# Attention A of a two-block transformer kernel: scores with the keys on partitions, plain fp32 values on column halves, values in portions of two key tiles

## What is computed

```python
qa = axial_rope(rms_norm(qa.reshape(b, s, A_HEADS, HEAD_DIM), q_norm_a), ...)
ka = axial_rope(rms_norm(ka.reshape(b, s, A_KV_HEADS, HEAD_DIM), k_norm_a), ...)
def block(qi):
    sc = jnp.einsum('bqkgd,bskd->bkgqs', qi, k).astype(jnp.float32) * scale
    p = jax.nn.softmax(sc, axis=-1).astype(v.dtype)
    return jnp.einsum('bkgqs,bskd->bqkgd', p, v)
oa = dense_gqa_attention(...) * jax.nn.silu(ga)
```

## Time and profile before

| | us |
|---|---|
| median of the runs | 2344.59 |
| the profiled execution | 2350.09 |
| its span, first to last instruction | 2348.8 |
| attention A, from its first matmul to the first of `pe_b_proj` | 190.0 |
| `pe_b_proj`, to the first matmul of attention B | 32.4 |

### The profile page before, as it was taken

How to read it: one execution, slowest core, us unless ns; L and a number is a source line. 1 busy time by engine, 2 the same in 40 slices (tenths; PEclk the granted TensorE clock), 3 DMA queues, 4 the chain that set the end, 5 groups by cost and what they waited for, 6 DMA issues and landing times.

```text
span 2348.8 us, 31548 instructions
## 1 busy us (share of the span) xinstructions
PE 2281.2 (97%) x11982; PEld 1881.3 (80%) x11982; DVE 1444.2 (61%) x1936; ACT 1113.2 (47%) x1804; POOL 963.3 (41%) x745
## 2 busy tenths in 40 slices
PE   5999999989999999999999999999999999999998
PEld 5888789968888888876688677888878888888886
DVE  6256499958886276248845773342876666666665
ACT  5222288878885155457734371321433333333334
POOL 1111256446662237862122121122265566655551
PEclk8999999999999999999999999999999999999999
DMA  8255300010002133210031311031111111111111
GB/s 315 77 154 161 116 6 1 1 37 1 1 1 108 45 111 108 90 73 2 10 126 51 117 45 37 28 117 45 55 54 54 54 53 48 48 51 54 54 54 72
DMA packets 156393, 154.85 MB, mean 66 GB/s; under 512 B 12550, under 2 KB 141620, under 8 KB 154324
## 3 DMA queue, kind: packets, MB, share of 16 engines
q1 hardware_dynamic: 156244, 152.84, 21.0%
HBM read 128.05 MB, written 20.97 MB: 63 GB/s over the span
## 4 chain that ended last, share of the span: by engine, by line
PE 82%; ACT 5%; DVE 4%; issue 3%; POOL 2%; DMA 2%; SPq 1%; ACTq 0%; DVEq 0%; POOLq 0%
PE ps L256 28%; PE ps L2903 15%; PE ps L2920 9%; PE ps L1630 6%; PE ps L1136 5%; PE ps L1159 4%; PE ps L1146 4%; PE ps L1940 2%; PE ps L1923 2%; PE ps L1909 2%; DMA MKW<-in_ada_w 1%; ACT B_PR L1220 1%; POOL WSL L2820 1%; ACT B_PTH L1214 1%; PE ps L2879 1%
## 5 line engine op out<-in xcount | busy, mean ns | idle before, releaser
L243 POOL TENSOR_TENSOR WL<-WR,WH 128x1024 fp32r<-128x1024 f32 (+2 forms) x71 | 163.0, 2297 | 653.7 <-ACT WH L238 653.6
L256 PE MATMUL ps<-HH,WH 128*128 128x512 f32 (+2 forms) x880 | 281.5, 401 | 1.0 <-POOL WL L243 0.6
L256 PE MATMUL ps<-HL,WH 128*128 128x512 f32 (+2 forms) x880 | 273.5, 392 | 0.0
L256 PE MATMUL ps<-HH,WL 128*128 128x512 f32 x848 | 263.2, 392 | 0.0
L3133 DVE TENSOR_TENSOR XF<-ps,XF 128x1024 f32<-128x1024 f32 x168 | 201.5, 1220 | 32.0 <-PE ps L2920 25.3
L2903 PE MATMUL ps<-HC,WSH 128*128 128x512 f32 x640 | 197.1, 389 | 0.0
L256 PEld LDWEIGHTS ps<-HL,WH 128*128 128x128 f32 (+2 forms) x880 | 164.7, 187 | 38.1
L256 PEld LDWEIGHTS ps<-HH,WH 128*128 128x128 f32 (+2 forms) x880 | 160.8, 188 | 39.1 <-issue 5.3
L256 PEld LDWEIGHTS ps<-HH,WL 128*128 128x128 f32 x848 | 160.3, 189 | 34.1
L1172 DVE TENSOR_REDUCE NM<-ps 128x1 f32<-128x1024 f32 x128 | 156.5, 1223 | 33.4 <-PE ps L1136 31.9
L2820 POOL TENSOR_TENSOR WSL<-WSR,WSH 128x512 fp32r<-128x512 f32 x100 | 131.5, 1315 | 106.1 <-ACT WSH L2814 105.4
(11 more groups left out here) (455 smaller groups left out, 5527.9 us busy)
## 6 DMA issues: line engine op xcount, KB each, us to landing
WS<-in_w_ffn_in SPq DMA_DIRECT2D x44, 512.0 KB, 5.1
MKW<-in_ada_w SPq DMA_DIRECT2D x32, 512.0 KB, 4.3
spill<-X SPq DMA_DIRECT2D x3, 4096.0 KB, 13.8
OW<-in_w_ffn_out SPq DMA_DIRECT2D x22, 512.0 KB, 3.4
...
```

The source lines that it names most:

```text
L243: pool.tensor_tensor(low[:, :, :], raw[:, :, :], high[:, :, :].bitcast(F32), ALU.subtract).then_inc(*w_low.up(t))
L256: last = pe.matmul(ps[0:w.out, 2 * s + h, :], wt[:, k, :], x[:, k, halves(h)], start=(k == 0 and n == 0), stop=(k == w.kt - 1 and n == len ...
```

## The change

Attention A gets programs of its own (`pe_turned`, `dve_turned`, `act_turned`, `pool_turned`). The work is cut into 8 units `u`, each with two heads (`e`) and 512 queries. For a unit:

- the look: 8 rounds of two matmuls with queries on partitions and the high part of q alone give approximate scores; VectorE's maximum over 1024 keys (`dve_t_top`) goes into one column of `TOP`. The looks of unit `u+1` are made during unit `u`; those of unit 0 stand in `pe_even_proj` at the eight places of `LOOKS`, in tiles `j` 16 and 17.
- `dve_t_wide` spreads the maxima to 128x512, `pe_t_turn` transposes them in four pieces, and ScalarE and VectorE copy one head each (`t_moved`) into the lower rows of the query operand `QB`, so that the second score matmul subtracts the maximum.
- the scores come out with keys on partitions, 128 keys by 512 queries, two matmuls for a key tile and a head, one PSUM bank for each head; ScalarE's exponential (128x512) writes plain fp32 `PT` that is used as it is: no transposes and no low part.
- the values: for a key tile two matmuls of plain fp32, 64 wide, on the two column halves (`pe_t_values`), in portions of two key tiles: parts 0 and 1 at `k` 5 and 7, parts 2 and 3 in the next unit at `k` 1 and 3.
- the row sums: GpSimd adds `PT[k]` for k = 1 to 5, VectorE for k = 6 and 7 (one unit later; in the last unit k = 4 to 7), 128x1024 each; two matmuls with ones (`pe_t_sums`) sum over partitions and spread the result, VectorE takes the reciprocal of 128x512 elements, and GpSimd multiplies (`pool_t_mixed`).

The queries' and keys' high and low parts are made in other places and by other engines (ScalarE for high parts; VectorE and GpSimd one low part each for two heads). In `pe_b_proj` the last unit's sums come between tile 0 and tile 1, and the first two tiles have new waits.

```diff
@@ -839,6 +840,13 @@
+            if (j, k) in LOOKS:
+                i = LOOKS.index((j, k))
+                if i == 0:
+                    pe.wait_ge(*q_high.at("A", 1, 1))
+                    pe.wait_ge(*t_rest.at("A", 0, "key"))
+                    pe.wait_ge(*rope_done.at(4))
+                pe_t_look(A, 0, i)
...
+    A.KS = two("A_KS", 75, 175.5, [P, SEQ])
+    A.PT = place("A_PT", 143.5, [P, TT, 2, HALF])
+    A.SUM = [place("A_SUM0", 183.5, [P, 2, HALF]), place("A_SUM1", 187.5, [P, 2, HALF])]
+    A.TOP, A.TOPW = place("A_TOP", 1.53125, [P, 2, TT]), place("A_TOPW", 120.5, [P, 4, 2, HD])
+    A.INV, A.GATED = place("A_INV", 124.5, [P, HALF]), place("A_GATED", 128.5, [P, HALF])
+    A.look = lambda u, e: (A.QA[u // 2 % 2][e][:, :], A.KS[u // 4])
+    A.passes = lambda u, e: ((A.KS[u // 4], A.QA[u // 2 % 2][e]), (A.KE[u // 4], A.QB[u // 2 % 2][e]))
+    A.shift = lambda u, e: A.QB[u // 2 % 2][e][HD:P, halves(u % 2)]
+    A.value = lambda u, k, e: VA[:, k, rows(u // 4, HD)]
...
+    def pe_t_look(D, u, i):
+        g, e, t, b = D.tag, i // 4, i % 4, t_look_bank(u, i)
+        if u == 0:
+            if i:
+                pe.wait_ge(*t_top.at(g, 0, i - 1))
+        elif u == 1 and i == 0:
+            pe.wait_ge(*t_top.at(g, 0, TT - 1))
+        elif u == 1 and i == 1:
+            for odd in range(2):
+                pe.wait_ge(*t_moved(odd).at(g, 0))
+        else:
+            pe.wait_ge(*t_top.at(g, *divmod(TT * u + i - 2, TT)))
+        q, keys = D.look(u, e)
+        c = 4 * (u % 2) + t
+        for j in range(2):
+            last = pe.matmul(ps[:, b + j, :], q[:, rows(c)], keys[:, halves(j)], start=True, stop=True)
+        last.then_inc(*t_seen.up(g, u, i))
...
+    def pe_t_scores(D, u, k):
+        g = D.tag
+        passes = [D.passes(u, e) for e in range(2)]
+        steps = [(n, e) for e in range(2) for n in range(len(passes[0]))]
+        if k == 0:
+            steps = sorted(steps)
+        for n, e in steps:
+            if n == 0 and (u or k):
+                pe.wait_ge(*t_exp.at(g, *((u, k - 1) if k else (u - 1, TT - 1)), e))
+            shifted = n == len(passes[0]) - 1
+            if shifted and k == 0:
+                if u and u % 2 == 0:
+                    pe.wait_ge(*D.lows_made(u, e))
+                pe.wait_ge(*t_moved(e).at(g, u))
+            keys, q = passes[e][n]
+            last = pe.matmul(ps[:, e, :], keys[:, rows(k)], q[:, halves(u % 2)], start=(n == 0), stop=shifted)
+            if shifted:
+                last.then_inc(*t_scored.up(g, u, k, e))
...
+    def pe_t_values(D, u, part):
+        g = D.tag
+        for k in range(2 * part, 2 * part + 2):
+            if k == 0 and u:
+                pe.wait_ge(*t_gated.at(g, u - 1))
+            pe.wait_ge(*t_exp.at(g, u, k, 1))
+            for e in range(2):
+                last = pe.matmul(ps[rows(e, HD), 2, :], D.value(u, k, e), D.PT[:, k, e, :], start=(k == 0), stop=(k == TT - 1))
+            last.then_inc(*t_used.up(g, u, k))
...
+    def pe_t_sums(D, u):
+        g = D.tag
+        if u == UNITS - 1:
+            pe.wait_ge(*t_top.at(g, u, TT - 1))
+        else:
+            for odd in range(2):
+                pe.wait_ge(*t_moved(odd).at(g, u + 1))
+        pe.wait_ge(*t_added(g, u, TT - 1))
+        for e in range(2):
+            last = pe.matmul(ps[rows(e, HD), t_sums_bank(u), :], D.ONES[:, :], D.SUM[u % 2][:, e, :], start=True, stop=True)
+        last.then_inc(*t_sums.up(g, u))
...
+    def pe_t_turn(D, u):
+        g = D.tag
+        pe.wait_ge(*t_wide.at(g, u))
+        if u >= 2:
+            pe.wait_ge(*t_inverse.at(g, u - 2))
+        for t in range(4):
+            last = pe.transpose(ps[:, t_shift_bank(u), rows(t)], D.TOPW[:, t, :, :].rearrange("p e n -> p (e n)"), IDENT[:, :])
+        last.then_inc(*t_turned.up(g, u))
...
+    def pe_turned(D, ready):
+        for u in range(UNITS):
+            for k in range(TT):
+                i = k if k < 4 else k + 1
+                if u + 1 < UNITS and i < TT:
+                    if i == 0 and u + 1 in ready:
+                        ready[u + 1]()
+                    pe_t_look(D, u + 1, i)
+                pe_t_scores(D, u, k)
+                if k == 3:
+                    if u + 1 < UNITS:
+                        pe_t_look(D, u + 1, 4)
+                if k % 2:
+                    part = (k // 2 + 2) % 4
+                    if part < 2:
+                        pe_t_values(D, u, part)
+                    elif u:
+                        pe_t_values(D, u - 1, part)
+                if k == 3 and u:
+                    pe_t_sums(D, u - 1)
+            if u + 1 < UNITS:
+                pe_t_turn(D, u + 1)
+        for part in range(2, 4):
+            pe_t_values(D, UNITS - 1, part)
...
+    def dve_t_wide(D, u):
+        g = D.tag
+        dve.wait_ge(*t_top.at(g, u, TT - 1))
+        if u:
+            dve.wait_ge(*t_turned.at(g, u - 1))
+        dve.tensor_copy(D.TOPW[:, :, :, :], D.TOP[:, u % 2, :].rearrange("p (e t) -> p t e", t=4).unsqueeze(3).to_broadcast(
+            [P, 4, 2, HD])).then_inc(*t_wide.up(g, u))
...
+    def add_t_part(eng, D, u, k):
+        g = D.tag
+        eng.wait_ge(*t_exp.at(g, u, k, 1))
+        if k == 1:
+            if u >= 2:
+                eng.wait_ge(*t_sums.at(g, u - 2))
+            if eng is pool:
+                pool_in_turn()
+            first = D.PT[:, 0, :, :]
+        else:
+            eng.wait_ge(*t_added(g, u, k - 1))
+            if eng is pool:
+                pool_in_turn()
+            first = D.SUM[u % 2][:, :, :]
+        eng.tensor_tensor(D.SUM[u % 2][:, :, :], first, D.PT[:, k, :, :], ALU.add).then_inc(
+            *(t_part if t_by_pool(u, k) else t_rest).up(g, u, k))
...
+    def dve_turned(D, beside):
+        for u in range(UNITS):
+            dve_t_moved(D, u)
+            more = u + 1 < UNITS
+            for i in range(4 * more):
+                dve_t_top(D, u + 1, i)
+            if u:
+                for k in range(6, TT):
+                    add_t_part(dve, D, u - 1, k)
+            if more:
+                dve_t_top(D, u + 1, 4)
+            beside(u, 0)
+            if more:
+                dve_t_top(D, u + 1, 5)
+            if u:
+                dve_t_gated(D, u - 1)
+            if more:
+                dve_t_top(D, u + 1, 6)
+            if u:
+                dve_t_inverse(D, u - 1)
+            if more:
+                dve_t_top(D, u + 1, 7)
+                dve_t_wide(D, u + 1)
+            beside(u, 1)
+        for k in range(4, TT):
+            add_t_part(dve, D, UNITS - 1, k)
+        dve_t_gated(D, UNITS - 1)
+        dve_t_inverse(D, UNITS - 1)
...
+    def act_turned(D, beside):
+        g = D.tag
+        for u in range(UNITS):
+            act.wait_ge(*t_turned.at(g, u))
+            act.activation(D.shift(u, 0), ps[D.shift_from(0), t_shift_bank(u), :], ACT.Copy).then_inc(*t_even_moved.up(g, u))
+            for k in range(TT):
+                for e in range(2):
+                    act.wait_ge(*t_scored.at(g, u, k, e))
+                    if u and e == 0:
+                        act.wait_ge(*t_used.at(g, u - 1, k))
+                        act.wait_ge(*t_added(g, u - 1, k))
+                    act.activation(D.PT[:, k, e, :], ps[:, e, :], ACT.Exp).then_inc(*t_exp.up(g, u, k, e))
+                if k % 4 == 3:
+                    beside(u, k // 4)
...
+    def pool_turned(D, beside):
+        for u in range(UNITS):
+            for k in range(1, TT):
+                if t_by_pool(u, k):
+                    add_t_part(pool, D, u, k)
+                if k == 3:
+                    beside(u)
+            if u:
+                pool_t_mixed(D, u - 1)
+        pool_t_mixed(D, UNITS - 1)
...
     def pe_b_proj():
-        pe.wait_ge(*e_done.at("A", N - 1))
         pe.wait_ge(*uv_low.at())
         for i, t in enumerate(B_PROJ):
+            if i == 0:
+                for e in range(2):
+                    pe.wait_ge(*t_exp.at("A", UNITS - 1, TT - 1, e))
+            elif i == 1:
+                pe_t_sums(A, UNITS - 1)
+                pe.wait_ge(*t_gated.at("A", UNITS - 1))
+                pe.wait_ge(*t_inverse.at("A", UNITS - 2))
             high, low = (CKH, CKL) if B_PARTS[i][0] == "k" else (CQH, CQL)
             pe_tile(t, high, low)
...
+            if i == 0:
+                act.wait_ge(*t_added("A", UNITS - 1, TT - 1))
```

More of the change, by code:

```diff
@@ L1280, in pool_dense, with t_moved @@
                 beside(s)
-    UV, UVH, UVL = (place("UV", 204, [P, B_HEADS * HD]), place("UVH", 44.5, [P, B_HEADS * HD], F32R),
+    t_seen, t_scored, t_exp, t_used, t_even_moved = ot_done, s_done, e_done, pv_done, h_out
+    t_turned, t_sums = t_done.steps("turned", "sums")
+    t_top, t_wide, t_odd_moved, t_gated, t_inverse, t_rest = l_out.steps("top", "wide", "moved", "gated", "inverse", "rest")
+    t_part, t_mixed = pool_made.steps("t_part", "t_mixed")
+    def t_moved(e):
+        return t_odd_moved if e else t_even_moved
@@ L1283, in build @@
```

(73 more changed lines are left out.)

120 lines of the change are left out of this document (83 added, 37 removed).

## The result

The changed kernel takes 2378.46 us (median of four runs, 2374.81 to 2379.4), the kernel before 2344.39 beside it: a ratio of 1.0149 (95% interval 1.0133 to 1.0165), 34 us slower. I had forecast 13 us slower, 2357.6, with a range of 2324 to 2374. The sign was right, the size too small, and the time lies outside the range. The spans of the two profiled executions (2348.8 before, 2378.1 now) differ by 29.3 us.

What follows compares the result with a forecast made beforehand. PE, busy 97%, was taken to bound the kernel. The changed stretch, 47.6 us plus six unit periods of 26.0, gave 203.6 against 195.2: 8 slower, plus 5 for half clock, 13 slower, median 2357.6; range 2324 to 2374.

Steps and rivals of the forecast that it cites:

- The wait for the additions: Attention A units: VectorE's additions taking turns with GpSimd last 2.7 to 3.4 us instead of 1.2; PE idles some 5 us.
- The end of a unit: Attention A: PE finishes scores and values at about 17.5 us, then waits 2 us for the spread maxima.
- more than 85%: Sign against the forecast: PE busy above 85% in attention A, where about 75% was expected.
- 8 value pairs x 0.43 = 3.4: PE's value products in an attention A unit: 3.4 us of its 16.4; bounds for a pair 0.43 and 0.86.
- my sum: Attention A to next stage's tile 2: looks 3.6, first unit 17.4, six unit periods, tail 26.6; 203.6 us against 195.2.
- few collisions: Rival, attention A: VectorE slips between GpSimd's additions; unit period (P) 21.4 us, 19 us faster, 2325; chance 0.22.
- PE sets the time: Rival, attention A: PE's work alone sets the unit period (P), 16.4 us; 49 us faster, 2296; chance 0.03.
- The half clock: Six middle units: PE runs at half speed behind each wait for additions; 5 us in all, bounds 0 and 13.
- a cold tensor engine: Rival, attention A: half clock holds 9 us and more behind each wait; 2366 to 2378 us; chance 0.15.
- The reciprocal: VectorE's reciprocal of 128x512 in each unit: 3.7 us, from 7 ns a column; bounds 0.69 and 3.7.
- The tail's wait for GpSimd: Next stage after attention A: weight tile 2 waits 4 to 6 us for GpSimd, replacing a wait of 0.93.
- two value pairs, and only then look 2: PE's order early in an attention A unit: two value pairs precede look 2, done 4.9 us behind the transposes.

## Why the prediction was right in sign and too small

- **The wait for the additions: right.** VectorE's additions that take turns with GpSimd's, PE's sums behind them, the looks behind those. The forecast named 2.7 to 3.4 us for an addition and about 5 us of idle PE a unit; it is 2.9 (5.86 for two) and 3.87. Moving two additions took 30 us away, so PE's wait behind this collision is the largest single cost of the change.
- **The end of a unit: wrong.** The forecast had PE wait 2 us there for the spread maxima. No middle unit has that wait, and VectorE waits for PE instead. PE is busy for 178.2 of the 207.7 us of attention A, 86%, where I had 75% and named more than 85% as a sign of being wrong. A unit came near the forecast by luck: I had 24.4 us for even units and 27.6 for odd ones before the half clock, and they take 27.2 and 27.8 to 28.1 with it.
- **The step that failed: "8 value pairs x 0.43 = 3.4".** I read six plain fp32 matmuls in 2.84 us and six pairs in 1.52 from the earlier trace rows, and took records for matmuls. Line L2269 has four matmuls in the program (two `m`, two `h`), and its whole run in the trace of before, of which the row shows the first part, is

```profile
1305.45 3.70 PE L2269 MATMUL ps<-CV,BD 128*128 128x512 f32 x8 [1.09 <-DVE CV L2528]
```

  eight records for four: a plain fp32 matmul has two, 0.43 each, so 0.86. The x12 of L1940 are three pairs, not six. The pair of 512 columns costs 0.9, about as much as one plain fp32 matmul over the whole array (0.86), so the halves do run together. The value 0.86 stood as my upper bound, for halves that don't, and I dismissed it by the same miscount. A portion of two key tiles is 1.9 us, not 0.9 and the change of shape. In the first unit, where PE sets the time, that is two portions, 1.8 us (19.2 for 17.4); in the last, six portions, 5.6 of 6.2; in the middle ones PE's wait covers most of it (the run with half of the products gains 0.8 us a unit). It comes through where look 2 stands behind part 2: I had that look done 4.9 us behind a unit's transposes, and in units 1 and 2 it is done at 6.3 and 5.7. That run comes within 2 us of each part of my sum. Put right, this term adds 7.4 us at the two ends; with the tail's half clock below, the forecast would have been some 23 us slower. The six middle units are another 4.4 over it (165.4 for 161).
- **My range didn't hold it** because the price of the value products entered no bound of the sum: PE's unit was 16.4 by my count, so it seemed to have 5 us of room. It is 21 to 22 (129.4 us of busy time in the stretch of six units when the additions were moved), as long as VectorE's without collisions. The rival "few collisions" (P = 21.4) would have been at PE's limit too, and the rival "PE sets the time" (P = 16.4) could not happen at all.
- **The half clock: right** in the middle units: taken at 5 us, 5.7 in the run that takes it away. The rival "a cold tensor engine", 2366 to 2378, is nearest to the measured 2378.5 by its number, but its condition, a half clock of 9 us and more behind each wait, did not come: it was 3 us.
- **The reciprocal: right,** 3.35 us for 3.7. The estimate of 4.3 us from the Trainium skill (VectorE: DVE Perf Modes, First, the fixed hardware budget) was further off. The tail's wait for GpSimd is 4.06 (4 to 6 forecast), but I left out the half clock behind it (a granted clock of 0.58 from 506 to 513): 2.4 us, in a stage that I had called unchanged.
- **What I did not ask:** what the portion's size does beside its changes of shape. The forecast had "two value pairs, and only then look 2" in its timetable, without asking how it would run with look 2 first. By the runs, that one place is worth 29 us (26 between the marks of the six middle units).

The costs aren't additive: additions moved (30), part 2 moved (29) and portions of four (30) each remove most of the same wait of PE.

## What to carry to other kernels

Before a price is read from a run of records, count the instructions of one line in the program against its records in the trace, for each type: here one number off by two made PE look as if it had 5 us of room in a unit. Where an engine waits for a result of another, the work that stands before the wait is part of the schedule: put the long independent work directly before the wait, and not where it delays what the other engine needs first. And operations of VectorE and GpSimd with all operands in SBUF are to be placed in each other's gaps before any is moved between the engines.

## What the runs showed beyond that

- Additions of 1.2 us cost 1.2 or 2.9, as they fall into GpSimd's gaps or not; a copy of 0.43 us cost up to 2.52 in the same way. When VectorE comes just as GpSimd's operation ends, two additions take 4.5 us; when it comes 1.5 us earlier, 5.9.
- A wait of 3.87 us on PE was followed by some 3 us at half clock, one of 0.84 us by none.
- The reciprocal of 512 columns takes 3350 ns; against the 155 ns of two columns in the earlier trace rows that is 6.3 ns a column, where the narrow ones gave 7.
